# Rounded weights and their remainders interleaved element by element in one tile, in a two-block transformer kernel

## The reference

```python
# first block
mod = silu(c) @ w_ada + b_ada
h = rms_norm(x, norm1_w) * (1 + scale1) + shift1
q, k, v, xBC, z, dt_raw, gates = split(h @ w_in)
attn = block_attention(q, k, v);  ssd = ssd_mixer(xBC, z, dt_raw, ...)
x = x + gate1 * ((g_attn * (attn @ w_attn_out) + g_ssd * (ssd @ w_ssd_out)) @ w_o)
x = x + gate2 * (square(relu(h2 @ w_mlp1)) @ w_mlp2)
# second block
dq, dk, dv, sq, sk, sv = split(u @ w_in_2)
x = x + concat(diff_attention(...), stick_breaking_attention(...)) @ w_out_2
x = x + (silu(u2 @ w_gate_2) * (u2 @ w_up_2)) @ w_down_2
```

## Time and profile before

| | |
|---|---|
| median of 3 runs | 922.19 us |
| lowest and highest | 919.66 and 927.25 us |
| span of the profiled execution | 926.9 us |
| the run that lies nearest to that span | 927.25 us |
| instructions | 18052 |

### The profile page before, as it was taken

The page is one execution under the profiler, slowest core; times in us unless marked ns, Lnnn a source line. Parts: engine busy times, 40 slices in busy tenths (PEclk is TensorE's granted clock), DMA queues, the critical chain, the costliest instruction groups (busy, mean ns, idle before and its releaser), DMA issues.

```text
span 926.9 us, 18052 instructions
## 1 busy us (share of the span) xinstructions
PE 903.5 (97%) x7424; PEld 859.7 (93%) x7424; DVE 668.4 (72%) x918; ACT 512.5 (55%) x696; POOL 79.8 (9%) x56
## 2 busy tenths in 40 slices
PE   5999999999999999999999999999998999999998
PEld 3899998788888899999999999988898999999998
DVE  6877998997699988778766545555875856666642
ACT  2566666667878773445655443346576754444430
POOL 0133000010465330000000000000000000000000
PEclk9999999999999999999999999999999999999999
DMA  9764554766322237684755555544332435555650
GB/s 376 302 242 151 204 192 147 263 219 236 124 65 87 92 138 250 223 301 146 264 182 182 186 188 193 192 152 169 116 126 86 142 137 187 185 190 193 217 192 18
DMA packets 25084, 168.00 MB, mean 181 GB/s; under 512 B 2868, under 2 KB 4532, under 8 KB 5048
## 3 DMA queue, kind: packets, MB, share of 16 engines
q1 hardware_dynamic: 23760, 164.90, 50.4%
q10 hardware_dynamic: 1256, 2.12, 0.6%
HBM read 165.95 MB, written 1.06 MB: 180 GB/s over the span
## 4 chain that ended last, share of the span: by engine, by line
PE 78%; DVE 8%; ACT 7%; issue 3%; DMA 3%; POOL 0%; SPq 0%; DVEq 0%; ACTq 0%; POOLq 0%
PE bank L1864 77%; DVE wlo L1107 2%; ACT whi L573 2%; DMA raw<-w_stream 2%; DVE acc L1152 1%; DMA adas<-w_stream 1%; ACT kw__113 L822 1%; PE bank L2132 1%; DVE eb L1432 1%; ACT ew L789 0%; DVE sslo L1468 0%; DVE wlo L1117 0%; DVE cvt L1341 0%; DVE p L1319 0%; ACT prob L724 0%
## 5 line engine op out<-in xcount | busy, mean ns | idle before, releaser
L1864 PE MATMUL bank<-hhi,whi 128*128 128x256 f32 (+1 forms) x1364 | 384.5, 284 | 0.8 <-DVE hlo L1210 0.6
L1864 PE MATMUL bank<-hlo,whi 128*128 128x256 f32 (+1 forms) x1352 | 377.5, 280 | 0.0
L1864 PE MATMUL bank<-hhi,wlo 128*128 128x256 f32 (+1 forms) x1352 | 375.7, 280 | 0.0
L1107 DVE TENSOR_TENSOR wlo<-raw,whi 128x2048 fp32r<-128x2048 f32 (+1 forms) x130 | 299.0, 2301 | 101.1 <-ACT whi L573 99.2
L573 ACT ACTIVATE whi<-raw 128x2048 fp32r<-128x2048 f32 (+1 forms) x132 | 250.6, 1898 | 101.3 <-PE bank L1864 74.2
L1864 PEld LDWEIGHTS bank<-hhi,whi 128*128 128x128 f32 (+1 forms) x1364 | 256.3, 188 | 11.5 <-issue 10.4
L1864 PEld LDWEIGHTS bank<-hlo,whi 128*128 128x128 f32 (+1 forms) x1352 | 257.2, 190 | 0.1
L1864 PEld LDWEIGHTS bank<-hhi,wlo 128*128 128x128 f32 (+1 forms) x1352 | 253.6, 188 | 0.0
L1864 PE MATMUL bank<-fhi,whi 128*128 128x256 f32 x432 | 121.4, 281 | 0.0
L1864 PE MATMUL bank<-flo,whi 128*128 128x256 f32 x432 | 121.4, 281 | 0.0
L1864 PE MATMUL bank<-fhi,wlo 128*128 128x256 f32 x432 | 121.4, 281 | 0.0
(11 more groups left out here) (296 smaller groups left out, 1311.2 us busy)
## 6 DMA issues: line engine op xcount, KB each, us to landing
raw<-w_stream SPq DMA_DIRECT2D x147, 1024.0 KB, 4.9
adas<-w_stream SPq DMA_DIRECT2D x8, 1024.0 KB, 8.6
xres<-x_t SPq DMA_DIRECT2D x1, 1024.0 KB, 10.1
out<-oute SPq DMA_DIRECT2D x8, 128.0 KB, 3.4
tabs<-tabs_in_dram ACTq DMA_DIRECT2D x1, 641.0 KB, 8.5
tabs<-tabs_in_dram ACTq DMA_DIRECT2D x1, 512.0 KB, 3.7
hankel<-bucket_rows ACTq DMA_DIRECT2D x1, 512.0 KB, 10.9
cols<-cols_in_dram ACTq DMA_DIRECT2D x1, 325.0 KB, 8.0
```

The costliest lines, as they stand in the source:

```text
L1107: nc.vector.tensor_tensor(out=wlo[:, c % RING, 0:n], in0=raw[:, r % RING, 0:n], in1=whi[:, c % RING, 0:n].bitcast(f32), op=ALU.subtract)\
L1864: return nc.tensor.matmul(out, lhsT, rhs, start=start, stop=stop)
```

## The change

The two tiles `whi` and `wlo` become one tile, `wsp`, with a last dimension of two. `whi` is its even elements, `wlo` its odd ones. Every instruction that wrote or read `whi` or `wlo` stays, with the same waits and the same number of elements. The step from one element to the next within a partition is now 8 bytes in place of 4. The new tile takes as many bytes as the two had together and stands where they stood, so no other tile moves. Within it the place of a ring slot changes: slot r of both now lies at 16 KB times r.

```diff
     raw = place("raw", [P, RING, CW], f32)
-    whi = place("whi", [P, RING, CW], f32r)
-    wlo = place("wlo", [P, RING, CW], f32r)
+    wsp = place("wsp", [P, RING, CW, 2], f32r)
+    whi, wlo = wsp[:, :, :, 0], wsp[:, :, :, 1]
     csil = place("csil", [P, KD], f32)
```

## The result

The change makes the kernel 2.6% slower: 948.88 us median (947.04 to 950.14, 4 runs) beside 923.78 us for the kernel before (919.66 to 927.25, 4 runs), a ratio of 1.0256 with a 95% interval of 1.0198 to 1.0313. The profiled execution took 949.0 us with a span of 947.2 us, 20.3 us above the span before.

What follows compares the result with a forecast made beforehand. The prediction took TensorE's stream of matmuls, paced by its weight loads, to bound the kernel. Its three terms, for loads, ACT and DVE, were each zero, so the forecast stayed at the median of 922 us, range 904 to 1000 us.

Steps and rivals of the forecast that it cites:

- first rival: Slower, chance 0.21: all 6324 loads at line 1864 pay for the step; about 1600 us if doubled, 941 at 3 ns.
- likeliest case: The whole kernel shows no change, chance 0.57: 915 to 931 us.
- (a): Weight loads from the tile, 6324 of 7424, reading over 1024 bytes: taken as zero, at most 107 ns more per load.
- Step (b): ACT's copy to `whi`, written with a step of 8 bytes: taken as zero, at most 2.05 us per split.
- Step (c): DVE's difference, reading `whi` and writing `wlo` with the step: taken as zero, at most 2.05 us per split.
- second rival: Slower, chance 0.15: DVE and ACT pay for the step, up to 2.05 us per split; about 986 us.
- Third: Faster, chance 0.04: the distance between loads locks at 113 ns everywhere, 16 us gained, 906 us.
- fourth rival: A little slower, chance 0.03: the distance between loads locks at 117.6 ns everywhere, 14 us lost, 936 us.

Runs made afterwards that it cites:

- the kernel with the writes alone: Changed kernel, with loads reading 128 contiguous elements of the interleaved tile while ACT and DVE still write with a step of two: 928.75 us, ratio 0.997.
- the one with the places alone: Changed kernel with the tile's last two dimensions exchanged: `whi` and `wlo` contiguous again, ring slots at their new places: 929.23 us, ratio 1.0038.
- the first kernel of small groups: Kernel before plus 320 matmuls behind the first q chunk, in groups of 32 at steps 1 to 16, narrow then wide; total time not given.

## Why the prediction was wrong

The forecast was no change, 922 us, and the kernel is 2.6% slower. The time lies inside the range, which held the first rival's small form, but the likeliest case was the wrong one. The prediction's own sign for a wrong (a) is what came: the loads' means are up, and in gu (746 to 860 us) the distance is 119.7 ns, above 118.

**What bounds the kernel** was read rightly. TensorE's stream set the time before and after, the load was the half of the pair without room (112 ns by itself), and the warning that even a few ns would show was the right one: it gave 941 us for 3 ns per load.

**Step (a) failed**, the term taken as zero. The prediction put it so: "So a read over 1024 bytes in 107 ns is something that the memory already gives TensorE." The moving side's rate was carried over to the weight load, and the load is another reader: 118 ns at a step of two against 111 to 112. So the term was too small by 6 to 7 ns in 112. (The 107 ns is itself a little under what the rows give: 54 to 57 ns for 64 columns are 108 to 114 for 128.) The doubled time taken as the upper bound does exist, at a step of 16 bytes: 234 ns per load, 1657.55 us for the kernel, near the 1600 us written down for it.

**"Any ns added to the reading of 128 weights is added to the distance"** was right for part of the stream only. From 96 to 144 us 6.5 ns came through. In the late stretches 2 did: there the stream already ran at 117.6 ns, 5 to 6 ns above what the contiguous load needs by itself and about what the stepped one needs (118). 3334 loads at 2 ns and at most 2990 at 6.5 ns give 7 + 19 = 26 us as an upper bound, against 20.3 us between the spans.

**Step (b)**, ACT: not zero but 0.21 us per split, and hidden, as the kernel with the writes alone shows (0.997). **Step (c)**, DVE: zero as forecast. The upper bound of 1.0 ns per element from the two reductions was sound for their step of 32 bytes: 0.75 to 0.8 ns for DVE were measured at 16 and 32 bytes. So the second rival had a true price for a step that this change doesn't have.

**Third and fourth rival**, the paces. The profiles of the kernel before and of the one with the places alone show the same stretches at different paces, while all their runs together do not differ (1.0038). But the pace of 120 ns that came is neither of the two. The steadiness of the changed kernel (947.04 to 950.14 us in 4 runs, where the kernel before goes over 19 us in 51) fits with there being only one pace. That this is the reason is not shown; the granted clock was steadier in these four runs too (0.996 to 1.000 against 0.987 to 1.000).

## What to carry to other kernels

Before a layout puts a step into an operand, count the elements that fall in 16 bytes: with two float32 DVE doesn't notice, ACT pays 4% in the small copies and 11% in the kernel's, and a weight load pays some 6%. With one, DVE pays about half as much again, ACT 60%, and a weight load takes twice as long. And ask of each reader whether it has room: here ACT's 27 us more were free and TensorE's 6 ns were not. A stream of load and matmul pairs that runs about as fast as its loads alone (113 against 112 ns here) has none, and a rate seen on one side of the pair is no evidence for the other.

## What the runs showed of the hardware that was not expected

- The same stream of loads and matmuls runs at 113 or at 117.6 ns, in the same kernel at different places, and at the same place in kernels that differ only in where the ring slots lie or in the order of the products. Neither of these changed the time. What chooses the pace is open.
- One stepped load among contiguous ones delays the matmuls behind it by about 20 ns in all, three times its own 6 to 7 ns, while a stream of nothing but stepped loads loses no more than one with every third stepped.
- A step of three elements costs between: 174 ns, halfway from 118 to 234.
- At steps of 4, 8 and 16 elements a load takes 234, 238 and 217 ns at a granted clock of 0.50, no more than at the upper level (234, 238 to 242 and 221 ns).
- Narrow matmuls (2 to 10 columns), back to back, came with a fall of the granted clock to the lower level though TensorE was never idle: 0.54 on average from 46 to 49 us in the first kernel of small groups. Twelve at a time behind 24 wide ones ran at 1.00 at steps 1 to 3; the wide ones behind the groups at steps 4 and 8 had 0.61 (66 to 69 us) and 0.57 (72.3 to 75.6 us).
